# Input tiles 1 to 4 of a two-layer transformer step: loaded as 32x32 squares by GpSimd's queue and transposed by VectorE, in place of TensorE transposes

## The reference

```python
def _even_layer(x, pos, caches, prm, lam_init):
    h = x @ w_in
    q_lat, ckv, krope, g_mla, dq, dk, dv, g_diff = _split_cols(h, EVEN_SECTIONS)
    q = (_rmsnorm(q_lat, q_g) @ w_uq).reshape(b, s, MLA_HEADS, MLA_QK_DIM)
    ...
    ckv = _rmsnorm(ckv, kv_g)
    krope = _rope(krope, pos, MLA_ROPE_DIM, MLA_ROPE_THETA)
    ...
    o = jnp.concatenate([o_mla * jax.nn.silu(g_mla), o_diff * jax.nn.silu(g_diff)], axis=-1) @ w_out
    y = _layernorm(ALPHA * x + o, ln_g, ln_b)
```

## Time and profile before

| | us |
|---|---|
| median of 3 runs | 826.94 |
| lowest, highest | 826.76, 828.35 |
| the profiled execution | 827.74 |
| its span in the trace | 826.0 |
| TensorE busy in it | 799.8 |
| VectorE busy | 530.2 |
| ScalarE busy | 408.9 |
| GpSimd busy | 74.8 |

### The profile page before, as it was taken

The page is one execution under the profiler, slowest core; times in us unless marked ns, Lnnn a source line. Parts: engine busy times, 40 slices in busy tenths (PEclk is TensorE's granted clock), DMA queues, the critical chain, the costliest instruction groups (busy, mean ns, idle before and its releaser), DMA issues.

```text
span 826.0 us, 16906 instructions
## 1 busy us (share of the span) xinstructions
PE 799.8 (97%) x6588; PEld 702.6 (85%) x6588; DVE 530.2 (64%) x1055; ACT 408.9 (50%) x935; POOL 74.8 (9%) x102
## 2 busy tenths in 40 slices
PE   7999999999999999999999999999999999999994
PEld 6997798998889998778999988888888888887673
DVE  4576266565666567576822765676566776778877
ACT  4133533444445555432325556665567565687710
POOL 2120011000000000002210110001000100121002
PEclk9999999999999999999999999999999999999998
DMA  7732121211423334331332433333423433344203
GB/s 242 167 97 65 52 64 56 68 47 40 143 90 93 117 122 135 124 109 70 121 123 77 130 103 117 101 101 125 143 82 97 131 122 117 105 131 131 69 24 128
DMA packets 67533, 86.25 MB, mean 104 GB/s; under 512 B 6016, under 2 KB 53920, under 8 KB 67456
## 3 DMA queue, kind: packets, MB, share of 16 engines
q1 hardware_dynamic: 63712, 74.47, 29.2%
q0 software_dynamic: 3744, 10.70, 4.1%
HBM read 74.25 MB, written 10.90 MB: 103 GB/s over the span
## 4 chain that ended last, share of the span: by engine, by line
PE 81%; issue 8%; DVE 4%; ACT 3%; POOL 2%; DMA 0%; SPq 0%; DVEq 0%; POOLq 0%; ACTq 0%
PE turn L967 25%; PE pair L967 17%; PE proj L967 16%; PE value L967 15%; PE turn L1016 3%; PE turn L1201 2%; PE value L1016 1%; POOL rstd L940 1%; PE proj L1016 1%; ACT w_words L1401 1%; PE proj L1201 1%; DVE probs L1754 1%; DMA x_sb<-in_x_prompt_dram 0%; PE pair L1016 0%; DVE w_words L1635 0%
## 5 line engine op out<-in xcount | busy, mean ns | idle before, releaser
L1635 DVE TENSOR_TENSOR w_words<-stage,w_words 128x512 fp32r<-128x512 f32 (+1 forms) x136 | 91.9, 682 | 93.5 <-ACT w_words L1401 93.2
L967 PE MATMUL turn<-w_words,xT_hi 128*128 128x256 f32 (+2 forms) x712 | 150.4, 308 | 1.0 <-DVE xT_lo L1640 0.7
L967 PEld LDWEIGHTS turn<-w_words,xT_hi 128*128 128x128 f32 x712 | 114.2, 191 | 6.2 <-DVE x_sb L1886 1.5
L967 PE MATMUL turn<-w_words,xT_lo 128*128 128x256 f32 (+2 forms) x364 | 108.8, 299 | 0.0
L1401 ACT CAST w_words<-stage 128x512 fp32r<-128x512 f32 (+1 forms) x144 | 87.1, 616 | 28.9 <-DMA stage<-in_w_in_even_dram 14.4
L967 PE MATMUL proj<-w_words,xT_hi 128*128 128x256 f32 (+2 forms) x380 | 76.6, 300 | 0.0
L967 PE MATMUL turn<-xT_hi,w_words 128*128 128x320 f32 x320 | 74.9, 314 | 0.0
L967 PE MATMUL pair<-w_words,xT_hi 128*128 128x512 f32 (+2 forms) x272 | 71.7, 350 | 0.1
L967 PEld LDWEIGHTS turn<-w_words,xT_lo 128*128 128x128 f32 x364 | 69.4, 191 | 2.5
L967 PE MATMUL value<-w_words,xT_hi 128*128 128x256 f32 (+2 forms) x316 | 69.8, 315 | 0.4 <-DVE w_words L1635 0.4
L1754 DVE TENSOR_TENSOR_SCAN probs<-probs 128x512 f32<-128x512 f32 (+4 forms) x80 | 61.4, 801 | 1.6
(11 more groups left out here) (520 smaller groups left out, 1709.7 us busy)
## 6 DMA issues: line engine op xcount, KB each, us to landing
stage<-in_w_in_odd_dram SPq DMA_DIRECT2D x64, 256.0 KB, 2.7
stage<-in_w_in_even_dram SPq DMA_DIRECT2D x44, 256.0 KB, 2.9
k_c<-in_cache_sb_k_dram SPq DMA_DIRECT2D x32, 256.0 KB, 3.6
v_c<-in_cache_sb_v_dram SPq DMA_DIRECT2D x32, 256.0 KB, 2.9
mlaK<-in_cache_diff_k_dram SPq DMA_DIRECT2D x8, 512.0 KB, 4.0
mlaK<-in_cache_diff_v_dram SPq DMA_DIRECT2D x8, 512.0 KB, 4.5
stage<-in_w_out_even_dram SPq DMA_DIRECT2D x16, 256.0 KB, 2.8
stage<-in_w_out_odd_dram SPq DMA_DIRECT2D x16, 256.0 KB, 2.7
```

The source lines that it names most:

```text
L967: return nc.tensor.matmul(o, l, r, start=first, stop=last)
L1635: v.tensor_tensor(piece(w_lo[:, sec % 2, words]), piece(stage[:, n % STAGES, :]), piece(w_hi[:, sec % 2, words].bitcast(F32)), ALU.subtrac ...
```

## The change

Tile 0 of x is handled as before. For tiles 1 to 4 SP's four loads of 512 KB are dropped, and so are TensorE's transposes and their PSUM banks. GpSimd's queue waits for the right half of tile 0 (`x_right_in`), then issues for each tile four loads, one for each group of 32 partitions, ahead of its small loads. Load j brings the 32 columns 32j to 32j + 31 of each feature block of all 128 rows: 1024 runs of 128 bytes, 128 KB. Partition 32j + r receives rows 4r to 4r + 3. A new job `("xq", t, h)` lets VectorE transpose the 32x32 squares of half a tile from `x_sb` into `x_turn`, which lies in the space of `mlaK`, unused until the latT jobs. ScalarE's copy and VectorE's subtraction then read `x_turn` in place of the bank, and TensorE waits for the subtraction by a semaphore of its own, `xlo_done`. In the list the jobs of tile 1 now stand ahead of A(0); the places of the others stay.

```diff
--- before.py
+++ after.py
@@ -57,6 +57,7 @@
 GW = GH * HD
 DIFF_ROWS = DH * 2 * NEW
 QUAD = 2 * NEW
+SQ = 32
 
 
 
@@ -215,9 +216,9 @@
     first, second = convert("A0"), convert("A1")
 
     def layer0(t):
-        return [("xT", 0, t, 0), ("xT", 0, t, 1)]
-
-    jobs = [("xT", 0, 0, 0)] + first[:1] + [("xT", 0, 0, 1)] + first[1:] + [("A", 0, 0)] + layer0(1)
+        return [("xq", t, 0), ("xq", t, 1), ("xT", 0, t, 0), ("xT", 0, t, 1)]
+
+    jobs = [("xT", 0, 0, 0)] + first[:1] + [("xT", 0, 0, 1)] + first[1:] + layer0(1) + [("A", 0, 0)]
     jobs += layer0(2) + second[0:1] + [("A", 1, 0)] + layer0(3) + second[1:2] + [("A", 2, 0)]
     jobs += layer0(S_TILE) + second[2:3] + [("A", 3, 0)] + second[3:4] + [("A", S_TILE, 0)]
     jobs += flat_jobs(beside([[("A", t, 1)] for t in tiles], convert("dv0"))) + [("rms",)]
@@ -385,12 +386,17 @@
     return []
 
 
+def squares(job):
+
+    return job[:2] == ("xT", 0) and job[2] > 0
+
+
 def assign_banks(schedule):
 
     first = next(i for i, j in enumerate(schedule) if j[0] == "score")
     uses, turns, holder, where = {s: 0 for s in SLOTS}, {}, {}, {}
     for i, job in enumerate(schedule):
-        ring = RING_OF.get(job[0])
+        ring = None if squares(job) else RING_OF.get(job[0])
         begun = where.get(("begin", job[1], job[3])) if job[0] == "out" and job[2] == 2 and job[4] else None
         if begun:
             where[job] = begun
@@ -525,6 +531,7 @@
         dk_c, dv_c = caches[:, 0], caches[:, 1]
         dk_cT = vm[:, :, :].rearrange("p a b -> p (a b)").rearrange("p (s h k) -> p s h k", s=2, h=DH)
         sq = flat(dkT)
+        x_turn = flat(mlaK).rearrange("p (t k n) -> p t k n", t=TILES - 1, k=KD)
         l0.close()
 
 
@@ -566,6 +573,7 @@
         hi_done, cvt_done = sem("hi_done"), sem("cvt_done")
         pool_cvt_done = sem("pool_cvt_done")
         xhi_done = sem("xhi_done")
+        x_turned, xlo_done = sem("x_turned"), sem("xlo_done")
         upper_read = sem("upper_read")
         subln_done = sem("subln_done")
         ocvt_hi, ocvt_done = sem("ocvt_hi"), sem("ocvt_done")
@@ -664,6 +672,8 @@
                       if j[0] == "stats" or (j in ends and (j[1],) + j[3:] not in stats_later)]
         stats_no = {j: i + 1 for i, j in enumerate(stats_jobs)}
         gate_no = ordinal(("sig",))
+        turned_no = ordinal(("xq",))
+        xlo_no = ordinal(("xT",), squares)
         two_parts_no = ordinal(("xT", "ogT"))
         ocvt_no = ordinal(("mcvt", "ocvt", "otile"))
         silu_jobs = [j for j in schedule if j[0] in ("G", "gd")]
@@ -694,6 +704,8 @@
         wo = [a["w_out_even"].rearrange("a k c -> (a k) c"), a["w_out_odd"].rearrange("a k c -> (a k) c")]
         x_p = a["x_prompt"].rearrange("b (t p) d -> p (b t) d", p=P)
         x_s = a["x_sample"].rearrange("b q d -> (b q) d")
+        x_squares = [a["x_prompt"].rearrange("b (t r m) (k p) -> (b t) r (m k) p", t=PT_TILES, r=SQ, p=P)[t] for t in range(PT_TILES)]
+        x_squares.append(x_s.rearrange("(r m) (k p) -> r (m k) p", r=SQ, p=P))
         ckv_cache = a["cache_mla_ckv"].rearrange("a b (h p) c -> p (a b) h c", p=P)
         kr_cache = a["cache_mla_krope"].rearrange("a b (h p) c -> p (a b h) c", p=P)
         dk_cache = a["cache_diff_k"].rearrange("a b (h p) n i d -> p (a b) h (n i d)", p=P)
@@ -746,12 +758,8 @@
             sp.dma_start(x_sb[:, 0, D // 2:], x_p[:, 0, D // 2:]).then_inc(x_right_in, 16)
             for n in range(1, STAGES):
                 load_quarter(n)
-            for t in range(1, TILES):
-                src = x_p[:, t, :] if t < PT_TILES else x_s
-                sp.dma_start(x_sb[:, t, :], src).then_inc(x_in[t], 16)
-                if t == 1:
-                    sp.wait_ge(cvt_done, 1)
-                    load_quarter(STAGES)
+            sp.wait_ge(cvt_done, 1)
+            load_quarter(STAGES)
 
             def load_diff_k(b):
                 sp.dma_start(dk_c[:, b % 2, :, :], dk_cache[:, b, :, :]).then_inc(dk_in[b % 2], 16)
@@ -880,7 +888,11 @@
         def _(pool):
             nc.gpsimd.memset(minus_half[:, :], -0.5).then_inc(pool_step, 1)
             pool.wait_ge(pool_step, 1)
-            pool.wait_ge(x_in[PT_TILES - 1], 16)
+            pool.wait_ge(x_right_in, 16)
+            for t in range(1, TILES):
+                for j in range(P // SQ):
+                    rows = slice(j * SQ, (j + 1) * SQ)
+                    pool.dma_start(x_sb[rows, t, :].rearrange("r (n c) -> r n c", c=SQ), x_squares[t][:, :, rows]).then_inc(x_in[t], 16)
             pool.dma_start(probs[:, 0, 0:MASKS], a["c_masks"]).then_inc(small_in, 16)
             for buf, name in ((sel, "c_sel"), (sign, "c_sign")):
                 pool.dma_start(buf[:, :], a[name]).then_inc(small_in, 16)
@@ -993,6 +1005,13 @@
                 if units[sec][0] == job:
                     wait_split(pe, QUARTERS * SECTIONS.index(sec) + quarter)
 
+            def wait_x(t, h):
+
+                if t:
+                    pe.wait_ge(xlo_done, xlo_no[("xT", 0, t, h)])
+                else:
+                    wait_drained(pe, ("xT", 0, t, h))
+
             def project(job, t):
 
                 wait_bank(pe, job)
@@ -1001,7 +1020,7 @@
                     for k in range(KD):
                         wait_quarter(job, sec, k // 2)
                         if job[0] == "A" and k == KD // 2:
-                            wait_drained(pe, ("xT", 0, t, 1))
+                            wait_x(t, 1)
                         if job[0] in TWO_SUMS:
                             m = two_sums(ps(job), x_block(k, tok(t)), sec, k * HALF, n, k == 0, k == KD - 1)
                         else:
@@ -1030,6 +1049,8 @@
             for job in schedule:
                 kind = job[0]
                 done = filled[where[job][0]] if job in where else None
+                if squares(job):
+                    continue
                 if kind == "xT":
                     _, layer, t, h = job
                     if layer == 0:
@@ -1038,7 +1059,7 @@
                         pe.wait_ge(ln_done, ln_no[("ln", 0, t)])
                     transposes(job, [(i * P, x_sb[:, t, (4 * h + i) * P:(4 * h + i + 1) * P]) for i in range(4)])
                 elif kind == "A":
-                    wait_drained(pe, ("xT", 0, job[1], 0))
+                    wait_x(job[1], 0)
                     project(job, job[1])
                 elif kind in ("dq", "dk", "dv", "gd"):
                     project(job, job[1])
@@ -1382,7 +1403,12 @@
             for job in schedule:
                 kind = job[0]
                 done = drained[where[job][0]] if job in where else None
-                if job in two_parts_no:
+                if squares(job):
+                    _, _, t, h = job
+                    ks = slice(4 * h, 4 * h + 4)
+                    act.wait_ge(x_turned, turned_no[("xq", t, h)])
+                    nc.scalar.copy(xT_hi[:, ks, tok(t)], x_turn[:, t - 1, ks, :]).then_inc(xhi_done, 1)
+                elif job in two_parts_no:
 
                     dst, src = transposed(job)
                     wait_filled(act, job)
@@ -1622,7 +1648,19 @@
             for job in schedule:
                 kind = job[0]
                 done = drained[where[job][0]] if job in where else None
-                if job in two_parts_no:
+                if kind == "xq":
+                    _, t, h = job
+                    ks = slice(4 * h, 4 * h + 4)
+                    dve.wait_ge(x_in[t], 16 * (P // SQ))
+                    v.transpose(x_turn[:, t - 1, ks, :].rearrange("p k (r m) -> p k m r", r=SQ),
+                                x_sb[:, t, :].rearrange("p (m k c) -> p k m c", k=KD, c=SQ)[:, ks]).then_inc(x_turned, 1)
+                elif squares(job):
+                    _, _, t, h = job
+                    ks = slice(4 * h, 4 * h + 4)
+                    dve.wait_ge(xhi_done, two_parts_no[job])
+                    v.tensor_tensor(xT_lo[:, ks, tok(t)], x_turn[:, t - 1, ks, :], xT_hi[:, ks, tok(t)].bitcast(F32),
+                                    ALU.subtract).then_inc(xlo_done, 1)
+                elif job in two_parts_no:
 
                     dst, src = transposed(job)
                     dve.wait_ge(xhi_done, two_parts_no[job])
```

## The result

| | before | after |
|---|---|---|
| median, us (6 runs each, same chip) | 827.08 | 834.32 |
| lowest to highest | 826.76 to 828.71 | 833.57 to 834.97 |
| ratio, 95% interval | | 1.0082, 1.0069 to 1.0095 |
| the profiled execution, us | 827.74 | 834.97 |
| its span | 826.0 | 833.2 |

The change makes the kernel 7.2 us slower, 0.82%; forecast were 826.4 us and 823.3 to 830.7. The busy times say already that nothing heavy was added: TensorE's idle time in the span grew from 26.2 to 32.8 us, so nearly all of the loss is waiting. Aligning ScalarE's instructions of the two traces gives where: +3.9 us at dv0's first output (41.90 us before, 45.84 after), +4.7 at 60 us, +5.2 at 155 us, +5.8 at 187 us, +7.1 from 410 us to the end.

A forecast was written before the change was run, and what follows sets the result against it. TensorE, 97% busy, bounds the kernel: removing transposes saves at most 3.6 us, waiting for squares leaves 2.0, dv0's late weights 0.8, the RMS chain takes 0.3; sum -0.5, median 826.4 us, range 823.3 to 830.7.

The forecast's parts named there:

- The issue price: GpSimd's queue: each of sixteen square loads takes 0.84 us to issue, bounds 0.54 and 1.17.
- rival (b): GpSimd's queue: dearer issues drain it late, dv0's weights hold TensorE; 831.9 us at 1.17, deciding from about 0.87; chance 0.22.
- (c): Square loads: strided 128 B runs move slowly, tile 4 ready near 50 us, 851 in all; chance 0.08 with unforeseen slow transport.
- None of this bounds by itself; VectorE has the room, and at 1.4 us a transpose ... still hidden: VectorE: added transposes at 0.65 us each, bounds 0.5 and 1.4, hold nothing up; landing to TensorE takes 2.1 us.
- The squares' landing: Square loads of tiles 1 to 4: each lands 2.75 us after its issue begins.
- Quarter 0 comes through, the fourth is ready at 40.15: dv0's weights: first quarter loads before the repeating loads, last is ready at 40.15 us, so dv0 goes 0.8 us early.
- I price no change of TensorE's clock: TensorE before the A products: holes of about half a us, shorter than the present one, cost no clock change.
- The shift is carried to the end: After dv1: later stages follow each other by semaphores, so the -0.5 us shift stays to the end.

The follow-up runs named there:

- a_flat: The changed kernel with VectorE's transposes writing 32 consecutive words per square, tokens in another order; 832.24 us, ratio 1.0048 to the kernel before.
- a_norep: The changed kernel with the five small loads that repeat one row reading distinct rows instead; 834.15 us, ratio 1.0076 to the kernel before.
- b_late: The kernel before with GpSimd's small loads waiting for the split of weight quarter 5 instead of x tile 3; 832.23 us against 827.93, ratio 1.0056.
- a_fn: The changed kernel with transposes writing 32 consecutive words and the five row-repeating loads reading distinct rows; 831.74 us against 827.26 before, ratio 1.0058.
- a_fnp: The changed kernel with 32-word transpose writes, distinct rows for the five row-repeating loads, and 32 throwaway TensorE transposes; 829.67 us against 827.26 before, ratio 1.0030.
- a_sp: The changed kernel with the square loads issued on SP's queue and GpSimd's small loads waiting for tile 3; 837.59 us, ratio 1.0101 to the kernel before.
- a_early: The changed kernel without GpSimd's wait for the right half of x tile 0 ahead of the squares; 839.66 us, ratio 1.0146 to the kernel before.
- b_poolx: The kernel before with x tiles 1 to 4 as plain 512 KB loads on GpSimd's queue, small loads right behind; 829.00 us, ratio 1.0010.

## Why the prediction was wrong, step by step

- **The issue price was nearly right**: 0.79 us against 0.84 forecast. The masks at 19.62 against 19.6 are in part luck: the first issue was 0.8 us late, and sixteen shorter issues took that back. So rival (b), with its point of decision at an issue of 0.87, did not occur; the kernel got slower below that point. The transport at 128 B runs (c) was no disaster either: the last square had landed at 22.9 us, not near 50.
- **"None of this bounds by itself; VectorE has the room, and at 1.4 us a transpose ... still hidden" is the step that failed first.** The transpose took 1.0 us, inside its bounds, but I had worked out only the way from one tile's landing to TensorE (2.1 us) and not how often VectorE can do it. VectorE works its list in order: 4.3 us a tile against the product's 2.78. Even at 0.65 us a transpose the list is 3.6 (a_flat). A(4) started at 29.16 where 23.7 was forecast and 25.7 was the time before. From the start of tile 1's transposes to A(4) it took 15.3 us, where the forecast had 12.2: 3.1 of the 5.5 us. Together with the late squares of the next point, and with the weights eased, it costs +4.0 at dv0 (a_norep).
- **The squares' landing was mis-sized**: 4.8 and 4.2 us from issue against 2.75. Tile 1's transposes began at 13.86; forecast 8.7 + 2.75 = 11.5. That is the other 2.4 of the 5.5 us. The first issue at 6.99 in place of 6.2 is 0.8 of it. Tile 2 was complete at 17.9, forecast 14.8, just when VectorE came free, so a shorter list alone would not have started it sooner. My estimate added up one load by itself, while about six of them (4.8 / 0.79) and SP's weight loads shared the engines, whose share stood at 1.04 to 1.13 in the windows from 13.60 to 20.40. That the sharing is the reason is argued, not tried.
- **"Quarter 0 comes through, the fourth is ready at 40.15" failed as well.** After's first dv0 quarter waited until 39.35 and the fourth was split from 44.08. I had its load issued near 21.5 to 22, but the slot was freed by VectorE's late list, at 26.08, behind the repeating loads and not ahead of them; in b_late, where VectorE's list was not late, the load began at 21.70 and did come through. Kr_c landed at 39.1, forecast 37.5. So moving the small loads by +4.7 went with +6.3 for the fourth quarter; the mechanism of rival (b) was thus right, and its trigger came earlier than the 0.87. b_late, with loads later still and VectorE's list as before, shows +4.4.
- **The two brakes don't add.** 4.0 and 4.4 lie beside each other and come to 4.7 together: +3.9 at dv0 by VectorE's list, and 0.75 more when TensorE reaches the weight quarter that hangs on the RMS chain. That is why easing the weights alone (a_norep) gave back nothing that could be measured. Easing the transposes (a_flat) gave 2.8 us, in a run in which the weights came earlier as well.
- **"I price no change of TensorE's clock" failed in fact but cost little here.** I had called the 1.83 us ahead of A(1) a hole that the clock survived; the window shows that transposes filled it. With them gone TensorE stood idle for 2.8 us, and A(1) ran mostly at the 1.2 GHz level in place of 2.4 (0.57 granted), 4.4 us in place of 2.8. VectorE's list hid most of it; once that list is shorter, it shows (a_fn, a_fnp).
- **"The shift is carried to the end" failed**: 2.4 us were lost between 150 and 410 us, by no edit of the change but by the shorter instruction stream. No row that I had read could have given that number, but a shorter stream was certain, and a term for it belonged in the range.

## What to carry to other kernels

When work moves from a pacing engine to one with much idle time on average, add up the receiving engine's in-order list for one round of the pipeline and set it against the pacing engine's round; latency from input to output says nothing of it. A load moved to another queue is costed together with all that is queued behind it and all that shares the engines, and when two waits end near each other, each is measured with the other eased before either is blamed. Changing an instruction count can move the time by a few us far from the edit; a version padded to the old count tells that part from the rest.

## What the runs showed of the hardware

- VectorE's 128x512 fp32 transpose took 0.65 us where it wrote 32 words in a row and 1.0 us where each word stood 16 bytes from the last.
- A square load (1024 runs of 128 B, 128 KB) took 0.79 us to issue on GpSimd, where 128 runs took 0.54 and 2048 runs 1.17, and 0.74 in the median on SP (a_sp), where plain loads took 0.37 to 0.47: the price goes with the runs on either queue.
- Loads on SP's queue can be held up by GpSimd's packets: the fourth weight quarter of 256 KB took 14.7 us in a_early, in part behind two others of its own queue, 4.6 in b_poolx, and 3.0 in the kernel before. The Trainium skill ("DMA: Bandwidth & Descriptors", Queues, rings and completion order) has each engine alternate between the queues with work, packet by packet. a_early's trace agrees: from 7 to 22 us the queues moved 944 and 849 packets, nearly one for one, but 2.48 MB against 0.73.
- An instruction fetch is one packet of 16 KB, and beside it a load of 128 KB landed in 4.2 us in place of 2.9. The Trainium skill ("Runtime: NRT & Kernel Launch", Instruction fetch mechanics) calls the cost of crossing such a block mostly hidden. The kernel before agrees at the first of the three places, where the packet moved at 141.7 us, ahead of the load; in after, where packets fell on loads that TensorE waited for, the shift grew by 2.4 us at the three places.
